# A down projection in Strassen's manner: seven products of quarter blocks where there were eight

## The reference

```python
SEQ, D_MODEL, D_FF = 512, 1024, 2816

def conv_ffn(h, w_up, conv_w, w_down):
    up = causal_dwconv(h @ w_up, conv_w)          # conv over positions, 3 taps per channel
    gate, val = jnp.split(up, [D_FF], axis=-1)
    return (jax.nn.silu(gate) * val) @ w_down     # (512, 2816) @ (2816, 1024)

x = x + conv_ffn(rmsnorm(x, norm_ffn_g), w_up, ffn_conv_w, w_down)
```

## Time and profile before

| | |
|---|---|
| median of 3 runs | 1266.35 us (1266.24 to 1266.44) |
| the profiled execution | 1266.31 us, span 1264.6 us |
| TensorE clock granted | 0.999 |
| TensorE busy | 1248.1 us, 99% |
| VectorE, ScalarE, GpSimd busy | 66%, 46%, 18% |
| the first down projection | 752.43 to 817.71 us of the span |

### The profile page before, as it was taken

The page is one execution under the profiler, slowest core; times in us unless marked ns, Lnnn a source line. Parts: engine busy times, 40 slices in busy tenths (PEclk is TensorE's granted clock), DMA queues, the critical chain, the costliest instruction groups (busy, mean ns, idle before and its releaser), DMA issues.

```text
span 1264.6 us, 20146 instructions
## 1 busy us (share of the span) xinstructions
PE 1248.1 (99%) x6625; PEld 1003.2 (79%) x6625; DVE 832.9 (66%) x1709; ACT 581.1 (46%) x1053; POOL 223.6 (18%) x476
## 2 busy tenths in 40 slices
PE   8999999999999999999999999999999999999998
PEld 6777878878788788888888888888888776777776
DVE  6978777787787844434477773367764686794743
ACT  6664545545445432223344442244444455666632
POOL 2603304033140300001300000000004124440021
PEclk9999999999999999999999999999999999999999
DMA  6345363453634433333233323333224344333221
GB/s 184 83 118 127 85 156 89 119 126 82 151 93 122 121 107 90 100 100 100 84 101 100 100 75 100 111 97 100 81 83 109 102 114 122 83 86 98 83 68 67
DMA packets 283492, 130.01 MB, mean 103 GB/s; under 512 B 77296, under 2 KB 276271, under 8 KB 283445
## 3 DMA queue, kind: packets, MB, share of 16 engines
q1 hardware_dynamic: 283445, 129.42, 37.8%
HBM read 119.34 MB, written 10.06 MB: 102 GB/s over the span
## 4 chain that ended last, share of the span: by engine, by line
PE 93%; DVE 2%; ACT 1%; issue 1%; POOLq 0%; DVEq 0%; POOL 0%; ACTq 0%
PE gb L842 81%; PE gb L1290 2%; PE gd L1290 1%; PE gd L1240 1%; PE gd L1230 1%; PE gd L1218 1%; PE gd L943 1%; PE gd L1013 1%; PE gd L1024 1%; PE gd L935 0%; DVE wlo L1843 0%; PE gd L1197 0%; PE gd L1002 0%; PE gd L1001 0%; PE gd L1020 0%
## 5 line engine op out<-in xcount | busy, mean ns | idle before, releaser
L842 PE MATMUL gb<-act_a,whi 128*128 128x512 f32 x2656 | 888.5, 398 | 0.3 <-DVE wlo L1843 0.2
L842 PEld LDWEIGHTS gb<-act_a,whi 128*128 128x128 f32 x2656 | 498.9, 188 | 112.1 <-issue 10.0
L842 PE MATMUL gb<-act_a,wlo 128*128 128x512 f32 x1408 | 549.0, 390 | 0.0
L1843 DVE TENSOR_TENSOR wlo<-raw,whi 128x1024 fp32r<-128x1024 f32 (+1 forms) x197 | 236.0, 1198 | 137.4 <-ACT whi L1340 135.4
L1340 ACT ACTIVATE whi<-raw 128x1024 fp32r<-128x1024 f32 (+1 forms) x210 | 215.7, 1027 | 216.0 <-PE gb L842 190.5
L842 PEld LDWEIGHTS gb<-act_a,wlo 128*128 128x128 f32 x1408 | 265.1, 188 | 48.2 <-issue 0.5
L842 PE MATMUL gb<-act_b,whi 128*128 128x512 f32 x432 | 152.9, 393 | 2.0 <-DVE wlo L1843 1.3
L842 PEld LDWEIGHTS gb<-act_b,whi 128*128 128x128 f32 x432 | 81.1, 188 | 20.0 <-DVE wlo L1843 1.9
L2745 POOL TENSOR_TENSOR zs<-zs,ca 128x512 f32<-128x512 f32 x3 | 4.2, 1397 | 321.3 <-ACT ca L1343 321.3
L842 PE MATMUL gb<-act_b,wlo 128*128 128x512 f32 x128 | 49.9, 390 | 0.0
L2700 POOL TENSOR_TENSOR Ue<-Ue,elt 128x60 f32<-128x60 f32 (+14 forms) x120 | 45.0, 375 | 9.4
(11 more groups left out here) (494 smaller groups left out, 1496.9 us busy)
## 6 DMA issues: line engine op xcount, KB each, us to landing
raw<-in_w_in_dram SPq DMA_DIRECT2D x102, 512.0 KB, 3.8
raw<-in_w_up_dram SPq DMA_DIRECT2D x44, 512.0 KB, 3.7
raw<-in_w_down_dram SPq DMA_DIRECT2D x16, 384.0 KB, 3.2
raw<-in_w_down_dram SPq DMA_DIRECT2D x16, 320.0 KB, 3.0
raw<-in_w_a_out_dram SPq DMA_DIRECT2D x8, 512.0 KB, 4.0
raw<-in_w_b_out_dram SPq DMA_DIRECT2D x8, 512.0 KB, 3.5
raw<-in_w_o_dram SPq DMA_DIRECT2D x8, 512.0 KB, 3.5
raw<-in_w_out_dram SPq DMA_DIRECT2D x8, 512.0 KB, 3.5
```

Source lines behind the costliest of these rows:

```text
L842: ins = pe.matmul(gb[:, b, :], l, r, start=(first and m == 0), stop=(last and m == len(todo) - 1))
L1843: dve.tensor_tensor(wlo[:, i % 2, 0:k * P], raw[:, i % 4, 0:k * P], whi[:, i % 2, 0:k * P].bitcast(F32), ALU.subtract).then_inc(split_read ...
```

## The change

The first down projection (`f` = 0) is made otherwise. Let the tokens be cut into a first and a second half (256 each), the hidden blocks into even and odd ones, and the output blocks taken in pairs. For each of the 4 pairs this is a product of 2 x 2 by 2 x 2 blocks, and seven products P1 to P7 of quarter blocks take the place of eight. A product has 6 hidden blocks, 3 matmuls each, of 256 columns. Four of the seven use sums of weights (`SUM_OF`), which VectorE makes (`add_weights`, four for each pair, 768 columns each), and P4, P5, P6 (and P7, which shares with P6) use sums of tokens, which GpSimd makes (`token_sum`, four for each pair of hidden blocks) and cuts in high (ScalarE, `token_high`) and low (GpSimd, `token_low`, for the last pair VectorE). P6 and P7 are added in PSUM to P1, P3 to P5, so that VectorE adds every bank to `xT` in halves of 256 columns, P7 to both halves.

The order is P1, P5, P2, P6, P4, P3, P7 in the first pair and P1, P2, P4, P5, P6, P3, P7 in the others. The loads of a pair wait for all four weight sums of the pair before. The loops of the first up projection and of this down projection are written out on ScalarE, VectorE and, for the down projection, TensorE. Semaphores are renamed or shared, with no other wait by it.

```diff
+SEVEN = 7
+FIRST_PAIR = ("P1", "P5", "P2", "P6", "P4", "P3", "P7")
+OTHER_PAIR = ("P1", "P2", "P4", "P5", "P6", "P3", "P7")
+WEIGHTS_OF = {"P1": 0, "P2": 1, "P4": 3}
+SUM_OF = {"P5": 0, "P6": 1, "P3": 2, "P7": 3}
...
+                if f == 0:
+                    even_odd = w_dn_v[:, 0:FF_CUT[0], :].rearrange("p (k s) n -> p k s n", s=2)
+                    for p in range(KD // 2):
+                        for m, (q, s) in enumerate(DOWN):
+                            if p == 0:
+                                sp.wait_ge(split_ready, N_DN[0] + m - 3)
+                            else:
+                                sp.wait_ge(weights_added, 4 * p)
+                                used = [w for w, k in WEIGHTS_OF.items() if k == m]
+                                if used:
+                                    sp.wait_ge(split_ready, N_DN[0] + SEVEN * (p - 1) + pair_order(p - 1).index(used[0]) + 1)
+                            dst = raw[:, raw_at(p, m), 0:kh * P].rearrange("p (k n) -> p k n", k=kh)
+                            at = (2 * p + q) * P
+                            sp.dma_start(dst, even_odd[:, :, s, at:at + P]).then_inc(raw_landed[raw_at(p, m)], 16)
...
+            def seven(p):
...
+                for at, name in enumerate(order):
+                    n = N_DN[0] + SEVEN * p + at
+                    pe.wait_ge(hi_ready, n + 1)
+                    if name in read_first:
+                        pe.wait_ge(out_read, R_DN[0] + SEVEN * p + order.index(read_first[name]) + 1)
+                    bank = banks[into.get(name, name)][:, 0:HALF]
+                    for j in range(BLOCKS):
+                        if p == 0 and name in ("P1", "P2"):
+                            pe.wait_ge(up_lo, 2 * j + (1 if name == "P1" else 2))
+                        elif p == 0 and name == "P5":
+                            pe.wait_ge(pool_tiles, 1 + 3 * j + 1)
+                        elif p == 0 and name in ("P6", "P4") and j == BLOCKS - 1:
+                            pe.wait_ge(pool_tiles, 1 + 3 * BLOCKS - (1 if name == "P6" else 0))
+                        hi = whi[:, n % 2, j * P:j * P + P]
+                        pe.matmul(bank, hi, token_half(name, j, 0), start=(j == 0 and name not in into), stop=False,
+                                  skip_group_check=True)
+                        pe.matmul(bank, hi, token_half(name, j, 1), start=False, stop=False, skip_group_check=True)
+                    pe.wait_ge(split_ready, n + 1)
+                    for j in range(BLOCKS):
+                        ins = pe.matmul(bank, wlo[:, n % 2, j * P:j * P + P], token_half(name, j, 0), start=False,
+                                        stop=(j == BLOCKS - 1), skip_group_check=True)
+                    ins.then_inc(unit_done, 1)
...
+            def down_high(n):
+
+                p, name = down_set(n)
+                if name in WEIGHTS_OF:
+                    m = WEIGHTS_OF[name]
+                    sc.wait_ge(raw_landed[raw_at(p, m)], raw_count(p, m))
+                    src = raw[:, raw_at(p, m), 0:BLOCKS * P]
+                else:
+                    m = SUM_OF[name]
+                    sc.wait_ge(weights_added, 4 * p + m + 1)
+                    src = weight_sum(m)
+                sc.wait_ge(unit_done, n - 1)
+                sc.activation(whi[:, n % 2, 0:BLOCKS * P], src, ACT.Copy).then_inc(hi_ready, 1)
...
+            def down_out(n):
...
+                dve.wait_ge(unit_done, n + 1)
+                dve.wait_ge(out_read, R_DN[0] + n - N_DN[0])
...
+                dve.tensor_tensor(xj, xj, add, ALU.add).then_inc(out_read, 1)
+                if n + 2 < N_UP[1]:
+                    down_low(n + 2)
+                else:
+                    split(n + 2, n + 2)
+                at = n - N_DN[0] - SEVEN * p
+                if p == 0 and at in (2, 3):
+                    add_weights(at, 0)
+                elif p and at < 3:
+                    add_weights(at + 1, p)
+                if at == SEVEN - 1 and p < KD // 2 - 1:
+                    add_weights(0, p + 1)
...
+            for i in range(BLOCKS):
+                first_turn(i)
+            for n in range(N_DN[0] + 1, N_UP[1]):
+                down_out(n)
+                if n == N_DN[0] + 1:
+                    token_low("P6")
+                    token_low("P4")
...
+            for i in range(BLOCKS):
+                token_sum(0, i)
+                if i:
+                    token_low("P6", i - 1)
+                    token_low("P4", i - 1)
+                if i < BLOCKS - 1:
+                    token_low("P5", i)
+                for m in range(1, 4):
+                    token_sum(m, i)
```

More of the change, by code:

```diff
@@ L298, in flat, with token_half, token_sums, gated @@
             return t[:].rearrange("p c j -> p (c j)")
+        spare = ([act_a[:, 28 + n, :] for n in range(4)] + [act_b[:, 12 + n, :] for n in range(4)]
+                 + [gate_r[:, n, :] for n in range(8)] + [KT_r[:, n, :] for n in range(2)])
+        def token_half(name, i, low):
+            first, second = slice(0, HALF), slice(HALF, T)
+            even, odd = (slot((FF_LO if low else FF_HI) + 2 * i + q) for q in range(2))
+            both, last = spare[3 * i + low], spare[3 * i + 2]
+            return {"P1": even[:, first], "P5": even[:, second], "P2": odd[:, first], "P3": odd[:, second],
+                    "P6": both[:, first], "P7": both[:, second], "P4": last[:, second if low else first]}[name]
+        def token_sums(i):
+            at = 0 if i % 2 else 1024
+            return sums[:, at:at + 1024]
+        def gated(i):
+            return qc[:] if i % 2 else flat(Ui)
+        def weight_sum(m):
+            return sums[:, SUM_AT[m]:SUM_AT[m] + BLOCKS * P]
         def ring(g, what):
@@ L1145, in _ @@
                     ups(f, i, False)
-                if f == 1:
-                    down(1, 0, True)
+                if f == 0:
+                    for p in range(KD // 2):
+                        seven(p)
+                    continue
+                down(1, 0, True)
                 with pe.Fori(f, KD // 2) as i:
@@ L1652, in up_turn @@
+            for i in range(BLOCKS):
+                first_turn(i)
+            for n in range(N_DN[0] + 3, N_UP[1]):
+                down_high(n)
+                if n == N_DN[0] + 3:
+                    token_high("P6", BLOCKS - 1)
+                    token_high("P4", BLOCKS - 1)
+            behind[0] = LOADS_LESS
+            for n in range(N_UP[1], N_UP[1] + 2):
+                split(n, n)
+            for f in range(1, 2):
                 def up_turn(i, last=False):
@@ L1675, in _ @@
                     up_turn(FF_CUT[1] // 2 - 1, last=True)
[L1676 to L1680 removed]
+                if f == 1:
                     for j in range(KD):
@@ L2400, in down @@
                         split(N_DN[f] + 4 * i + 2 * q + 3, N_DN[f] + 2 * q + 3, next_k)
[L2402 to L2405, removed]
-                else:
+                if f == 1:
                     for j in range(KD):
```

206 lines of the change are left out of this document (179 added, 27 removed).

## The result

| | before | changed |
|---|---|---|
| median of 12 runs each, us | 1266.34 (1266.03 to 1266.78) | 1269.42 (1268.54 to 1270.13) |
| ratio, 95% interval | | 1.0024 (1.0016 to 1.0032) |
| profiled execution's span, us | 1264.6 | 1268.1 |
| TensorE clock granted | 0.999 | 0.999 |
| first matmul of the down projection to the first of the next up projection, us | 752.43 to 817.71: 65.28 | 752.33 to 820.78: 68.45 |

The forecast was 1265.2 us and a range of 1262.0 to 1269.3; the kernel came out 4.2 us above the one and 0.1 above the end of the other, which is less than its own runs lie apart. The stage alone is 3.17 us longer, of the span's 3.5, so the loss is inside it, and its first matmul starts where it did (752.33 for 752.43): the sums that GpSimd and VectorE got in the up projection don't delay the end of that stage.

The account below looks back on a forecast made before the run. TensorE bounds the kernel, streaming without a break. 4.8 us saved by the columns, less 3.1 given back in stalls and 0.6 to GpSimd, about 1.2 less than 1266.35: 1265.2 us, no change; range 1262.0 to 1269.3.

Parts of the forecast that it names:

- The pace: Down projection on TensorE: each 256-column matmul takes 120 ns by a fixed cost, so 504 take 60.5 us, 4.8 less.
- the reading by columns (113 ns): Rival for the down projection's matmuls: the excess goes with the columns, pace 113 ns, 1262.7 us; chance 0.34.
- a weight load that shows (from 130 ns): Rival in the down projection: weight load not hidden, 188 ns per matmul, some 25 us more, 1291; chance 0.07.
- The stalls of the first pair: TensorE waits in the down projection's first pair: 0.9 us in P5, 0.35 in P2, 0.35 before P7.
- GpSimd's hold: Entering the down projection, GpSimd's sums delay VectorE's chain twice, each 0 to 0.65 us; 0.6 taken in all.
- ... so the last at 20.0; ... P4 starts at 21.8: no stall: Second pair: four loads land 1.1 us apart, the last at 20.0 us, before P4 starts at 21.8; no stall.
- In later pairs the fourth sum comes earlier in the pair (after the third product), its loads land before P1 wants them, ... no stall: Pairs after the second: loads land before P1, low parts are ready 0.5 to 1 us before use; no stall.
- The sign that the prediction set for this: The forecast would be wrong if stalls in later pairs added up to more than 3 us.
- At the end ... stall 0.4: Start of next up projection: its first unit waits 2.5 us after P3 against P7's 2.16; stall 0.4 us.
- the two splits: High part on ScalarE, 1.06 us, and low part on VectorE, 1.23, after P3 for the next up projection.
- VectorE's queue becomes the bound: Rival: four products in a row with a sum take VectorE 2.75 us each; 4.1 us, 1269.3, slower; chance 0.17.
- P1 of the second pair: Stall of 1.1 us: its load, released by the first pair's fourth sum, gives the high part at 17.5 us.

## Why the prediction was wrong

**The pace: right.** 120.0 ns at 256 columns, so 60.5 us; the excess belongs to the matmul, and the reading by columns (113 ns) and a weight load that shows (from 130 ns) are both refuted. The Trainium skill ("TensorE: Matmul & The Clock Gate", section "Back-to-back issue gap") has 109 ns by its formula for an isolated matmul; the trace has 120, and it decides.

**The stalls of the first pair: right in place, P2's too small.** P5 1.07 for 0.9, P7 0.59 for 0.35, P2 1.22 for 0.35. The last two with the 0.6 for GpSimd's hold come to 1.3 against 1.8, so the mis-sized term is the hold: each was put at up to half of a GpSimd sum, twice, and the two operations on the path got 0.97 us together. With the sums cut P2's stall is 0.26 and P7's 0.39, near the 0.35 forecast for each. The mutual hold between VectorE and GpSimd that the Trainium skill has ("SBUF — State Buffer", "Who interferes with whom") is seen here: 1.39 and 1.22 us for 0.95 and 0.69.

**"... so the last at 20.0; ... P4 starts at 21.8: no stall", and "In later pairs the fourth sum comes earlier in the pair (after the third product), its loads land before P1 wants them, ... no stall": these steps failed.** P1's load is in time in the last two pairs, as forecast; P4's, the last of the four, is not in time in any. I counted the burst of four loads only once, for the second pair, with 3.2 us to the first landing and 1.1 for each further one, 6.6 after the sum. And for the later pairs I laid the sums out by TensorE's products, not by the loads that they themselves need. What the trace shows is a loop. After the fourth sum, at 767.1, SP issues four loads from 767.15 to 768.80, up to 0.63 apart. They share the rate and then trail off (windows; the last column is GB/s):

```profile
770.00:773.00 3.00, 1.76 (x14) 1.55 (x14) 1.30 (x2) 1.69 (x2) 0.00 (x0) 1.00 1.14 341
773.00:774.00 1.00, 1.00 (x11) 1.00 (x10) 1.00 (x2) 0.00 (x0) 0.00 (x0) 1.00 0.58 172
774.00:776.00 2.00, 2.00 (x19) 2.00 (x18) 0.54 (x2) 0.47 (x1) 0.00 (x0) 1.00 0.04 13
```

A load has landed when its semaphore has gone up by 16, in sixteen steps (`then_inc(..., 16)`). Of the last load's steps fifteen are there by 774.22 and the sixteenth at 775.51, and the second and third burst show the same (789.91 and 791.35, 805.84 and 807.06). In the gap little moves:

```profile
774.22:775.51 1.29, 1.29 (x13) 1.29 (x12) 0.00 (x0) 0.00 (x0) 0.00 (x0) 1.00 0.05 16
```

Fifteen of the sixteen come 7.1 us after the burst's first issue, 0.5 more than the forecast for all; the rest of the burst's excess is this one late step. Without it the loop would be 1.3 us shorter, by estimate 14.3 us, and fit into the pair.

ScalarE has P1's high part at 770.82 and P4's, whose load is the last, only at 775.53, 8.4 us after the first issue. VectorE's timeline goes on:

```profile
775.59 0.96 DVE L2544 TENSOR_TENSOR over_dec<-raw 128x768 f32<-128x768 f32 x1 [1.46 <-issue]
...
777.66 0.95 DVE L2544 TENSOR_TENSOR over_dec<-over_dec,raw 128x768 f32<-128x768 f32 x1
...
779.73 0.95 DVE L2544 TENSOR_TENSOR over_dec<-raw,over_dec 128x768 f32<-128x768 f32 x1
...
781.80 0.95 DVE L2544 TENSOR_TENSOR over_dec<-raw 128x768 f32<-128x768 f32 x1
```

The four sums stand 2.07 us apart, an eviction and a low part between each, and the next burst is issued at 782.77. From burst to burst it is 8.4 + 7.2 = 15.6 us, and 15.85 from there to the third (798.62), against 15.1 of TensorE's seven products. The loop of loads and sums is longer than the pair, so each pair waits, and no work of TensorE makes that up. The price of the second to fourth pair was 3.6 us where 1.1 was forecast: 1.50 instead of 1.1 at P1 of the second, 0.71 instead of nothing at its P4 and P3, and 1.35 instead of nothing in the last two. Cutting the loads (stage -4.4), cutting the sums (-2.6), or releasing each slot on its own and keeping the sums early (-4.5, the up projection's loads included) takes the loop apart; the first says that VectorE's queue is not the bound by itself. The sign that the prediction set for this, over 3 us of stalls in later pairs, did not show: its later pairs had 1.35, and the excess was spread over the terms of the balance below.

**"At the end ... stall 0.4": the second step that failed.** It counted the two splits and forgot SP's queue: the first load of the up projection stands behind the wait for the last pair's fourth sum. Issued at 814.64, it lets ScalarE begin at 818.41 and VectorE at 819.50, with TensorE through at 819.15 and going on at 820.78. With the loads let go slot by slot it is 0.48, near the 0.4 forecast.

**The rivals.** That VectorE's queue becomes the bound gave 1269.3 us, next to what was measured, by the wrong mechanism: with the loads taken away every sum and low part of the later pairs is still there, and none of their products waits. P3's 0.3 us in each pair is VectorE running late because its first sum was late. A sum just ahead of its high part, as that rival had it, shows only in the reordered kernels, with 0.26 to 0.58 per product.

**The balance.** Against the forecast: the first pair and the hold +0.7, P1 of the second pair +0.4, P4 and P3 of the second to fourth pair +2.1, the up projection +1.2, together 4.4, for 4.2 in the medians.

## What to carry to other kernels

When a load waits for the work on the data before it, and that work waits for loads, lay out the loop and compare its length with the time of the stage; a queue that waits for the last reader of all buffers instead of each buffer's own makes the loop as long as it can be. A sum can be late in two ways, as the gate of the next load and as the input of the next product, so moving it earlier for one may make it late for the other. And an eighth less columns is not an eighth less time where each matmul has a fixed part: of 65.3 / 8 = 8.2 us, 4.8 were there before the first stall.

## What the runs showed of the hardware

- A float32r matmul with its own 128x128 weight load costs its columns at 2.4 GHz and 13.3 ns: 226.7 ns for 512 columns, 120.0 for 256. The weight load is recorded with 0.19 us in both, longer than the 120.0 ns between two starts, so it overlaps the matmuls; whether a part of the 13.3 ns is its own no run here tells.
- After a wait TensorE's second matmul starts 0.22 us behind the first instead of 0.12 (0.19 in P3 of the later pairs): each stall costs 0.07 to 0.10 us beyond the wait.
- Four loads of 384 KB in a burst run at 341 GB/s, but the last, issued at 768.80, is there only 6.7 us later, at 775.53, against 3.2 for the median load before; in its last two microseconds almost nothing moves (13 GB/s). One of the load's sixteen completions comes 1.0 to 1.5 us behind the other fifteen in the last load of 16 of the 18 bursts in the six profiled kernels that issue them (the changed one, and those with the up projection's loads let go by slot alone, narrow GpSimd sums, narrow weight sums, the first pair's low parts swapped, its sum moved). In the five that release slot by slot none of the 60 loads shows it: their sixteenth comes at most 0.5 us late. What holds it up is open.
- A stall can have a second price, the clock. In the first of the two kernels with P5 ahead of P4 TensorE waited 1.5 us at P6 (after 0.7 at P5 and 1.0 at P2), and behind it the granted clock stood at the lower of its two levels, 1.2 GHz; 15 matmuls of 256 columns then started 0.213 us apart instead of 0.120, 1.3 us more. Its windows (column before last but one is the clock):

```profile
762.20:765.80 3.60, 3.56 (x17) 3.56 (x18) 3.58 (x6) 1.54 (x3) 1.24 (x33) 0.53 0.00 0
765.80:770.00 4.20, 4.20 (x38) 4.20 (x37) 3.08 (x6) 1.69 (x2) 0.00 (x0) 1.00 0.57 151
```

  The profiled execution of the kernel with narrow GpSimd sums shows the same behind its wait of 2.1 us before the up projection (822 to 824: clock 0.50), which explains 1.6 us of its 1270.94; behind the changed kernel's 1.6 us at that place, and behind the wait of 1.3 at P6 with the moved sum alone, the clock stayed at 1.00, and so it did behind 1.76 us at P1 of the second pair with the narrow weight sums. So the length of one wait doesn't decide it; what does is open. At the lower clock the starts lie 256 / 1.2 GHz apart, with no 13.3 ns on top.
